# PEER experts: an early score of the first tile, queries between the first expert groups, small last groups

## The reference, cut to what matters

```python
q = (xb @ w_q).reshape(n, PEER_HEADS, 2, PEER_HALF)
s = jnp.einsum('nhpq,hpkq->nhpk', q, sub_keys)
sv, si = lax.top_k(s, PEER_TOPK)
cand = sv[:, :, 0, :, None] + sv[:, :, 1, None, :]
...
cs, ci = lax.top_k(cand.reshape(n, PEER_HEADS, PEER_TOPK * PEER_TOPK), PEER_TOPK)
idx = jnp.take_along_axis(cand_idx.reshape(n, PEER_HEADS, -1), ci, axis=-1)
gate = jax.nn.softmax(cs.astype(jnp.float32), axis=-1).astype(xb.dtype)
ue = jnp.take(u_emb, idx, axis=0)
act = jax.nn.gelu(jnp.einsum('nhed,nd->nhe', ue, xb), approximate=False)
ve = jnp.take(v_emb, idx, axis=0)
return jnp.einsum('nhe,nhed->nd', gate * act, ve)
```

## Time and profile before

| | us |
|---|---|
| median of three runs | 2649.95 |
| profiled execution, its own time | 2655.38 |
| its span | 2653.7 |
| first gather issued | 1292.34 |
| TensorE's first expert group | 1317.17 |
| last expert group's first matmul | 2636.44 |
| TensorE busy | 2117.1 |
| VectorE busy | 1670.8 |
| ScalarE busy | 849.1 |

### The profile page before, as it was taken

One profiled execution on the slowest core, in us unless ns is written; L12 is line 12 of the kernel. 1 busy time (PEld: TensorE's weight loads), 2 busy tenths in 40 slices (PEclk: granted clock), 3 DMA queues, 4 the chain that ended last, 5 costly groups with the idle time before them and its releaser, 6 DMA issues.

```text
span 2653.7 us, 41107 instructions
## 1 busy us (share of the span) xinstructions
PE 2117.1 (80%) x16489; PEld 1345.7 (51%) x16489; DVE 1670.8 (63%) x3486; ACT 849.1 (32%) x1661; POOL 737.5 (28%) x607
## 2 busy tenths in 40 slices
PE   5899959974468998978789987777777778777876
PEld 2777737763468888856545543233333333332332
...
GB/s 175 146 205 251 245 200 162 83 215 1 49 180 158 111 134 137 36 177 110 267 420 417 408 393 415 415 420 420 421 420 420 421 420 420 420 420 421 421 420 209
DMA packets 131280, 742.05 MB, mean 280 GB/s; under 512 B 17392, under 2 KB 24592, under 8 KB 64528
## 3 DMA queue, kind: packets, MB, share of 16 engines
...
## 4 chain that ended last, share of the span: by engine, by line
DMA 30%; PE 13%; DVE 4%; issue 3%; ACT 2%; POOL 1%; POOLq 0%; DVEq 0%; ACTq 0%
DMA uvx<-in_uv_in,ic 27%; PE bank L2371 10%; DVE junk L2260 2%; DMA uv<-in_uv_in,ic 1%; POOL uvx L2097 1%; DMA scores_dram<-later 1%; PE bank L91 1%; PE bank L93 1%; PE bank L92 1%; ACT dg L2174 0%; PE bank L2352 0%; DVE wql L2226 0%; ACT ge L2169 0%; ACT L2169 0%; POOL uv L2097 0%
## 5 line engine op out<-in xcount | busy, mean ns | idle before, releaser
L2371 PE MATMUL bank<-uv,dg 128*128 128x512 f32 x1664 | 816.2, 648 | 208.5 <-ACT dg L2174 208.4
L2371 PEld LDWEIGHTS bank<-uv,dg 128*128 128x128 f32 x1664 | 335.3, 206 | 679.0 <-issue 404.6
L2097 POOL DMA_INDIRECT uv<-in_uv_in,ic x416 | 481.7, 1158 | 624.3 <-PE bank L2371 550.5
L2260 DVE SCALAR_TENSOR_TENSOR junk<-uv,gr 128x1024 f32<-128x1024 f32 x416 | 509.7, 1225 | 187.2 <-DMA uv<-in_uv_in,ic 157.7
L2169 ACT ACTIVATE ge<-dt_ 128x4 f32<-128x4 f32 x128 | 26.3, 205 | 946.5 <-DVE junk L2260 946.4
L2371 PE MATMUL bank<-uvx,dg 128*128 128x512 f32 x384 | 187.8, 646 | 57.5 <-ACT dg L2174 57.5
L2174 ACT ACTIVATE dg<-ident,gc_ 128x128 f32<-128x128 f32 x512 | 163.7, 390 | 29.4 <-DVE gc_ L2266 29.4
L91 PE MATMUL bank<-ht_hi,wh 128*128 128x256 f32 (+1 forms) x432 | 152.2, 352 | 22.9 <-DVE wl L587 22.9
L2371 PEld LDWEIGHTS bank<-uvx,dg 128*128 128x128 f32 x384 | 77.0, 206 | 168.2 <-issue 90.9
L2260 DVE SCALAR_TENSOR_TENSOR junk<-uvx,gr 128x1024 f32<-128x1024 f32 x96 | 117.7, 1226 | 59.9 <-DMA uvx<-in_uv_in,ic 57.1
L2097 POOL DMA_INDIRECT uvx<-in_uv_in,ic x96 | 112.6, 1173 | 124.0 <-PE bank L2371 114.2
...
## 6 DMA issues: line engine op xcount, KB each, us to landing
...
```

The lines of the kernel that those rows point to most:

```text
L2097: pool.indirect_dma_start(ring(i), None, g["uv_in"], bass.IndirectOffsetOnAxis(ap=ic[:, s % ICR, k:k + 1], axis=0)).then_inc(su[row_slot[i ...
L2260: dve.scalar_tensor_tensor(junk[:, :], ring(i)[:, 0:D], 1.0, hc[:, t % 2, :], ALU.mult, ALU.mult, accum_out=dt[:, k:k + 1]).then_inc(s_ud, 1)
L2371: mm = pe.matmul(acc(t, c)[:, :], dg[:, n % 2, k, :], ring(i)[:, D + 512 * c:D + 512 * c + 512], start=h == 0 and q == 0 and k == 0, stop= ...
```

## The change

**First scores.** A new path `first` makes head 0's query and scores for tile 0 alone: 2 halves x 8 slices x 2 products (with the high and with the low part of the tokens), 32 matmuls of 128 columns whose weights are the unsplit `wr`, into banks 6 and 7; then two score matmuls into bank 0. VectorE's `best(0)` waits for that score. Head 0's usual query and score follow for tiles 1 to 3, on 384 columns. The fetch of head 1's weights also waits until `first` has read head 0's.

**Order.** Only the queries of heads 0 and 1 stand ahead of the expert groups. Those of heads 2 and 3 follow one half after each group of pair 0, and score 2 follows the second group. ScalarE's copies and VectorE's splits move with them.

**The end.** The last pair's groups have 4, 4, 4, 2, 1 and 1 experts. The last tile's result is scaled, added and stored in two halves of 512 columns.

```diff
@@ -2038,6 +2039,8 @@
...
     NS = TT * HEADS
+    PARTS = [[GR] * NQ] * (NS - 1) + [[GR, GR, GR, GR // 2, GR // 4, GR // 4]]
+    START = list(itertools.accumulate([m for p in PARTS for m in p], initial=0))
     own = ExitStack()
...
@@ -2077,9 +2081,13 @@
...
         sp.wait_ge(s_res, t + 1)
-        sp.dma_start(outv[t], res).then_inc(s_out, 16)
         if t + 1 < TT:
+            sp.dma_start(outv[t], res).then_inc(s_out, 16)
             sp.dma_start(xr, x2_dram[t + 1]).then_inc(s_xr, 16)
+        else:
+            sp.dma_start(outv[t][:, 0:512], res[:, 0:512]).then_inc(s_out, 16)
+            sp.wait_ge(s_res, TT + 1)
+            sp.dma_start(outv[t][:, 512:D], res[:, 512:D]).then_inc(s_out, 16)
...
@@ -2107,6 +2115,8 @@
...
                     sp.wait_ge(s_lo, 2 * h - 1 + b)
+                    if h == 1:
+                        sp.wait_ge(s_fq, b + 1)
                     sp.dma_start(wr[:, b, :, :], g["wq_in"][2 * h + b].rearrange("p (k n) -> p k n", k=KT)).then_inc(s_wq[b], 16)
...
@@ -2141,7 +2151,8 @@
...
                     act.wait_ge(s_s, 2 * h)
-                act.activation(qt_[:, b, :], bank[2 + b][:, :], ACT.Copy).then_inc(s_qc, 1)
+                C = slice(0 if h else P, SEQ)
+                act.activation(qt_[:, b, C], bank[2 + b][:, C], ACT.Copy).then_inc(s_qc, 1)
                 if h + 1 < HEADS:
...
@@ -2149,28 +2160,35 @@
...
                     act.wait_ge(s_bt, h - SCR + 1)
-                act.activation(rt.sc[:, h % SCR, :, :], bank[4][:, 0:256].rearrange("p (a k) -> p a k", a=2), ACT.Copy).then_inc(s_sc, 1)
                 if h:
+                    act.activation(rt.sc[:, h % SCR, :, :], bank[4][:, 0:256].rearrange("p (a k) -> p a k", a=2), ACT.Copy).then_inc(s_sc, 1)
                     act.wait_ge(s_st, 16 * h)
-                act.activation(later[:, 0, :], bank[4][:, 256:512], ACT.Copy).then_inc(s_sc, 1)
+                act.activation(later[:, 0, :], bank[4][:, 256:512], ACT.Copy).then_inc(s_sc, 1 if h else 2)
                 act.wait_ge(s_s, 2 * h + 2)
...
+            def first():
+                for b in range(2):
+                    act.wait_ge(s_fq, b + 1)
+                    act.activation(qt_[:, b, 0:P], bank[6 + b][:, 0:P], ACT.Copy).then_inc(s_fc, 1)
+                act.wait_ge(s_fs, 1)
+                act.activation(rt.sc[:, 0, :, :], bank[0][:, 0:256].rearrange("p (a k) -> p a k", a=2), ACT.Copy).then_inc(s_fsc, 1)
+
             def exp(s):
...
             def gelu(n):
-                q = n % NQ
-                act.wait_ge(s_ud, GR * (n + 1))
+                k0, m = START[n] % TOPK, START[n + 1] - START[n]
+                act.wait_ge(s_ud, START[n + 1])
                 if n >= NQ:
                     act.wait_ge(s_gc, n - NQ + 1)
-                act.activation(ge[:, GR * q:GR * q + GR], dt[:, GR * q:GR * q + GR], ACT.Gelu).then_inc(s_ge, 1)
+                act.activation(ge[:, k0:k0 + m], dt[:, k0:k0 + m], ACT.Gelu).then_inc(s_ge, 1)
                 act.wait_ge(s_gc, n + 1)
                 if n >= 2:
-                    act.wait_ge(s_vd, GR * (n - 1))
-                for k in range(GR):
+                    act.wait_ge(s_vd, START[n - 1])
+                for k in range(m):
                     act.activation(dg[:, n % 2, k, :], ident[:, :], ACT.Copy, scale=gc[:, n % 2, k:k + 1]).then_inc(s_dg, 1)
...
@@ -2189,17 +2207,21 @@
...
             high(0, 1)
-            for h in range(3):
+            first()
+            for h in range(2):
                 query(h, 0)
...
                 score(h)
-                if h == 1:
+                if h == 0:
                     exp(0)
...
                 t, h = divmod(s, HEADS)
-                for q in range(NQ):
+                for q in range(len(PARTS[s])):
                     gelu(NQ * s + q)
-                    if q == 1 and s == 0:
+                    if s == 0 and q < 2:
+                        query(2, q)
+                    if s == 0 and q == 1:
+                        score(2)
                         exp(1)
...
@@ -2252,18 +2276,19 @@
...
                     dve.wait_ge(s_hc[t % 2], 16 * (t // 2 + 1))
-                for k in range(GR * q, GR * q + GR):
+                n = NQ * s + q
+                k0, m = START[n] % TOPK, PARTS[s][q]
+                for k in range(k0, k0 + m):
                     i = TOPK * s + k
...
                                              accum_out=dt[:, k:k + 1]).then_inc(s_ud, 1)
-                n = NQ * s + q
                 dve.wait_ge(s_ge, n + 1)
                 if n >= 2:
-                    dve.wait_ge(s_dg, GR * (n - 1))
-                dve.tensor_tensor(gc[:, n % 2, :], ge[:, GR * q:GR * q + GR], rt.pe[:, s % ICR, GR * q:GR * q + GR],
+                    dve.wait_ge(s_dg, START[n - 1])
+                dve.tensor_tensor(gc[:, n % 2, 0:m], ge[:, k0:k0 + m], rt.pe[:, s % ICR, k0:k0 + m],
                                   ALU.mult).then_inc(s_gc, 1)
...
@@ -2279,28 +2304,32 @@
...
                     dve.scalar_tensor_tensor(res[:, C], acc(t, n)[:, :], rs[:, 3:4], gt2b[:, C], ALU.mult, ALU.mult).then_inc(s_hx, 1)
-                dve.wait_ge(s_hx, 2 * t + 2)
-                dve.wait_ge(s_xr, 16 * t + 16)
-                dve.tensor_tensor(res, res, xr, ALU.add).then_inc(s_res, 1)
+                    if t == TT - 1:
+                        dve.wait_ge(s_hx, 2 * t + n + 1)
+                        dve.wait_ge(s_xr, 16 * t + 16)
+                        dve.tensor_tensor(res[:, C], res[:, C], xr[:, C], ALU.add).then_inc(s_res, 1)
+                if t < TT - 1:
+                    dve.wait_ge(s_hx, 2 * t + 2)
+                    dve.wait_ge(s_xr, 16 * t + 16)
+                    dve.tensor_tensor(res, res, xr, ALU.add).then_inc(s_res, 1)
...
                 low(0, b)
-            for b in range(2):
-                low(1, b)
             best(0)
...
             for b in range(2):
-                low(2, b)
+                low(1, b)
             gates(0)
+            low(2, 0)
             for s in range(NS):
                 t, h = divmod(s, HEADS)
-                for q in range(NQ):
+                for q in range(len(PARTS[s])):
                     dots(s, q)
-                    if s == 0 and q == 0:
-                        low(3, 0)
-                    if q == 1 and s + 3 < HEADS:
+                    if s == 0 and q < 3:
+                        low(*((2, 1), (3, 0), (3, 1))[q])
+                    if q == 1 and 0 < s and s + 3 < HEADS:
                         low(s + 3, 1)
...
@@ -2334,19 +2363,18 @@
...
                 for k in ks:
-                    mm = split_mm(pe, bank[2 + b][:, :], wh[:, b, k, :], wl[:, b, k, :], h2h[:, k, :], h2l[:, k, :],
+                    C = slice(0 if h else P, SEQ)
+                    mm = split_mm(pe, bank[2 + b][:, C], wh[:, b, k, :], wl[:, b, k, :], h2h[:, k, C], h2l[:, k, C],
                                   k == 0, k == KT - 1)
...
             def score(h):
-                if h == 0:
-                    pe.wait_ge(s_keys, 16)
                 pe.wait_ge(s_qc, 2 * h + 2)
...
                     pe.wait_ge(s_la, h)
-                for t in range(TT):
+                for t in range(0 if h else 1, TT):
                     for b in range(2):
...
@@ -2354,7 +2382,22 @@
...
-            for h in range(3):
+            def first():
+                for b in range(2):
+                    pe.wait_ge(s_wq[b], 16)
+                    for k in range(KT):
+                        for part in (h2h, h2l):
+                            mm = pe.matmul(bank[6 + b][:, 0:P], wr[:, b, k, :], part[:, k, 0:P].bitcast(FP32),
+                                           start=k == 0 and part is h2h, stop=k == KT - 1 and part is h2l)
+                    mm.then_inc(s_fq, 1)
+                pe.wait_ge(s_keys, 16)
+                pe.wait_ge(s_fc, 2)
+                for b in range(2):
+                    mm = pe.matmul(bank[0][:, NKEYS * b:NKEYS * b + NKEYS], qt_[:, b, 0:P], kt[:, b, :], start=True, stop=True)
+                mm.then_inc(s_fs, 1)
+
+            first()
+            for h in range(2):
                 query(h, 0)
...
@@ -2362,18 +2405,22 @@
...
                     pe.wait_ge(s_hx, 2 * (t - 1))
-                for q in range(NQ):
-                    for k in range(GR):
-                        n = NQ * s + q
-                        i = GR * n + k
+                for q in range(len(PARTS[s])):
+                    n = NQ * s + q
+                    for k in range(PARTS[s][q]):
+                        i = START[n] + k
                         pe.wait_ge(s_dg, i + 1)
...
                             mm = pe.matmul(acc(t, c)[:, :], dg[:, n % 2, k, :], ring(i)[:, D + 512 * c:D + 512 * c + 512],
-                                           start=h == 0 and q == 0 and k == 0, stop=h == HEADS - 1 and q == NQ - 1 and k == GR - 1)
+                                           start=h == 0 and q == 0 and k == 0, stop=h == HEADS - 1 and i % SLOTS == SLOTS - 1)
```

(6 more changed lines are left out.)

8 lines of the change are left out of this document (6 added, 2 removed).

## The result

The changed kernel takes 2653.32 us (median of 20 runs, 2647.50 to 2681.35), the kernel before, beside it, 2644.03 us (20 runs, 2637.20 to 2656.65). The ratio of the means is 1.0044, 95% interval 1.0025 to 1.0063 (that of the medians is 1.0035): slower by less than half a per cent, but clear of zero. The profiled execution took 2662.53 us, its span is 2660.8.

The account below looks back on a forecast made before the run. The loop over TensorE, ScalarE and VectorE paces heads 1 to 4, so head 1's entry counts, not the first gather alone. Head 1 9 us later less 3.4 at the end is 5.6 later: about 2656 us, range 2643 to 2665.

Parts of the forecast that it names:

- g4: Start of TensorE's fifth expert group, which opens head 1; claimed 12.6 us later than before.
- The first gather: GpSimd's first fetch of expert rows in head 0, claimed to leave at 1284.5, 7.8 us earlier.
- g0: Start of TensorE's first expert group, bound by the landing of head 0's score store; claimed 1307.6, 9.5 us earlier.
- g0 to g4: Starts of TensorE's first five expert groups, four steps through head 0; claimed 69.6 us with 5.1 of clock, against 47.5.
- Head 1: Delay with which head 1 goes on, carried to the end; worked out as 10.9 us, bounds 7.5 to 12.6, taken as 9.
- No backlog: DMA queue once in each head: hardly any transfers waiting, read from a landing 9.6 us after issue at head 2.
- The wait behind the score: TensorE from score to next group, 1373.31 to 1379.63: 6.32 us, of which the score is 1.8, the rest read as wait.
- The end: Last head's smaller groups and halved result; claimed gain 3.4 us: 3.1 groups, less 0.1 extra instruction, plus 0.4 shorter store.
- The sum: Whole kernel: 9 us later from head 1 less 3.4 at the end, so 5.6 us later, from a 2649.95 median.
- The lead kept: Rival: DMA engines pace everything from the first gather, so its 7.8 us lead is largely kept; 2642 us, chance 0.11.
- Late first scores: Rival: the new path's unsplit matmuls run at the lower clock throughout, lead 2.3 instead of 7.8; 2661 us, chance 0.09.
- TensorE slow through head 0: Rival: clock stays at 1.2 GHz through head 0's groups and queries; 32 us more, 2688, or 2672 with half; chance 0.07.

Follow-up runs that it names:

- e5_gelu: Changed kernel with TensorE's order kept, ScalarE's head 0 GELUs moved ahead of the query copies and VectorE's work there remixed; 1.0015 of the kernel before.
- e8_no_first: Changed kernel without the early scores, queries 0 to 2 ahead of group 0, query 3 in quarters between head 0's groups, GELUs before copies; 0.9985 of the kernel before.
- e6_spread: Changed kernel with three quarters of query 2 ahead of group 0, the rest and query 3 between later groups, GELUs moved earlier; 0.9951 of the kernel before.

## Why the prediction was right

The time, 2656 against 2653.32, held, and so did the mechanism up to g4; that the time came so near is in part luck, since two errors in it point in opposite directions. That about 0.5% is what a measurement can tell did not hold: the 20 runs put the change at 0.25 to 0.63% slower, clear of zero.

- **The first gather.** Predicted 7.8 earlier, came 6.5 earlier. The lower clock lasted until 1268.2, 5.3 us instead of 3, which is 1.0 of the 1.3 us.
- **g0.** Predicted 9.5 earlier, came 9.4 earlier. The store's landing set it as worked out, but the agreement hides two errors: the store was issued 1.6 later in the stage than I had it (at 24.9 instead of 23.3) and landed after 15.9 instead of 17.3; the split of query 1's low weights made TensorE wait 1.63 (1.8 in the sum).
- **g0 to g4.** Predicted 69.6, measured 70.0. The four steps were 15.3, 19.7, 15.3 and 14.2 with 5.1 of clock; they came as 18.0, 19.8, 17.9 and 14.3. The clock's share had its size but not its split: I took 1.7 three times, but two groups took 10.04 and 9.89, 2.8 to 2.9 over 7.13, and g1 nothing. g3 took 8.83, off the chain, because VectorE ended that step. The rows of the changed kernel show each group released behind a query's copy, and e5_gelu what that costs.
- **Head 1.** This term was mis-sized. The working gave 10.9 and I took 9, "on the low side of 10.9 because a wait of 2.83 was free". The 33rd gather came 11.3 later. The free wait was a chance: of two waits of 2.35, one was free and one was not.
- **No backlog.** This reading of the earlier trace rows was wrong, though it did no harm. I took 9.6 us from issue to landing for an empty queue. In the holes of the changed kernel, gathers land 5.4 to 5.8 us after their issue. So at head 2 the kernel before had some 4 us of transfers in hand, and head 1's entry 3.3 us earlier in e8_no_first did not bring the 33rd landing forward (it came 0.6 later). The 11.3 us of the changed kernel were more than that, and were carried: 10.1 at the landing of the 33rd gather, 11.1 at the 257th issue.
- **The wait behind the score.** The 6.32 us from 1373.31 to 1379.63 are not score and wait alone: a quarter of a query lies between, and the wait is 1.55. As a step from score to group on the chain, 6.32 held (6.41).
- **The end.** Predicted 3.4, measured 3.1 in the profiled execution, but 1.4 in the changed kernel's repetition. The sum had no clock in it, and the third group's did move it.
- **The sum.** 5.6 predicted; the last read came 8.1 later than before, 2.5 more, of which head 1 is 2.3 to 2.1. Against that, the level of 2649.95 lay 5.9 above the 2644.03 of the 20 runs. The 2.5 us too few and the 5.9 too many cancel in part: that is the luck.

**The rivals.** The lead kept: no, g4 came at 114.1 and the DMA engines had their holes, from 1345 to 1385 (I had them at 1345 to 1375), while VectorE waited for no gather in heads 1 to 4. With another order it would have been right in kind: e6_spread keeps the lead. Late first scores: VectorE started at 11.7 instead of 18.2, so no. TensorE slow through head 0: no, the mean granted clock was 0.90 in 1310 to 1375, where I had set 0.8, and 0.89 in that stretch before. The Trainium skill, "TensorE: Matmul & The Clock Gate", section "The HAM clock gate", says that the throttled state is the default and activity releases it; the trace agrees in the mean, and 0.50 shows in a stretch behind a wait (1345 to 1350). The table load and its GELU stood 1.30 apart again (1304.80 and 1306.10). The Trainium skill, "ScalarE: Activation LUTs", section "What ACT_TABLE_LOAD costs", gives 2.66 us for a switch; the trace doesn't show that here, and the 1.30 stands.

What I didn't ask was how good another order could be. The chain was most of the loss: e5_gelu, with TensorE's order kept, takes 8.3 of the 11.3 us at the 33rd gather away.
